# Modulation in plain fp32, four products side by side, with a new order of the first transfers, of the keys and of the second block

## The reference

```python
mod = silu(c) @ mod_w[l] + mod_b[l]           # and the same of c_ctx
shift, scale, gate = split(mod, 3)            # 1024 each
z = (rmsnorm(x, pre_g) * (1 + scale) + shift) @ w_in
y = three branches of z (attention of latents, pooling, gated linear attention)
x = x + gate * rmsnorm(merge(z, y) @ w_out, post_g)
...
x = x + rmsnorm(stick_breaking_and_relpos_attention(rmsnorm(x)))
x = x + rmsnorm(swiglu(rmsnorm(x)))
x = x + rmsnorm(recurrence(rmsnorm(x)))
x = x + rmsnorm(swiglu(rmsnorm(x)))
```

## Time and profile before

| | |
|---|---|
| median of 3 runs (lowest to highest) | 1644.01 us (1642.89 to 1644.77) |
| the profiled execution: time, span | 1642.83 us, 1641.0 us |
| TensorE busy, mean granted clock | 1507.7 us (92%), 0.963 |
| VectorE, ScalarE, GpSimd busy | 955.1, 770.3, 125.8 us |
| DMA | 212.57 MB, mean 130 GB/s |

### The profile page before, as it was taken

The page is one execution under the profiler, slowest core; times in us unless marked ns, Lnnn a source line. Parts: engine busy times, 40 slices in busy tenths (PEclk is TensorE's granted clock), DMA queues, the critical chain, the costliest instruction groups (busy, mean ns, idle before and its releaser), DMA issues.

```text
span 1641.0 us, 23866 instructions
## 1 busy us (share of the span) xinstructions
PE 1507.7 (92%) x9902; PEld 1308.2 (80%) x9902; DVE 955.1 (58%) x1522; ACT 770.3 (47%) x1212; POOL 125.8 (8%) x145
## 2 busy tenths in 40 slices
PE   6899999899999998999989886888999988889997
PEld 4767776787877775677988786877999988889997
DVE  5546875345453646576366557666566448767642
ACT  6534444432325354544535544565444358644342
POOL 0000000000000021000000013002122020122200
PEclk9999999899999999999999998999999999999999
DMA  9123333222222252322334454423666544446651
GB/s 369 64 64 116 128 103 116 77 78 77 77 77 96 84 181 85 97 90 69 99 121 137 154 185 154 131 77 103 207 192 186 187 142 142 141 149 186 193 182 63
DMA packets 58266, 212.57 MB, mean 130 GB/s; under 512 B 6384, under 2 KB 7536, under 8 KB 58032
## 3 DMA queue, kind: packets, MB, share of 16 engines
q1 hardware_dynamic: 56832, 205.29, 38.1%
q0 software_dynamic: 1328, 5.77, 1.1%
HBM read 209.98 MB, written 1.05 MB: 129 GB/s over the span
## 4 chain that ended last, share of the span: by engine, by line
PE 76%; DVE 13%; ACT 6%; DMA 3%; issue 1%; POOL 0%; SPq 0%; DVEq 0%; ACTq 0%; POOLq 0%
PE B L596 49%; PE B L612 7%; PE B L1005 7%; DVE WL L1785 4%; DMA RAW<-wstream 3%; PE B L719 3%; ACT WH L1200 3%; PE B L988 1%; PE B L1016 1%; PE B L799 1%; DVE M L2223 1%; PE B L786 1%; DVE X L2230 1%; PE B L621 1%; PE B L916 1%
## 5 line engine op out<-in xcount | busy, mean ns | idle before, releaser
L1785 DVE TENSOR_TENSOR WL<-RAW,WH 128x1024 fp32r<-128x1024 f32 x384 | 471.0, 1235 | 446.5 <-ACT WH L1200 445.5
L596 PE MATMUL B<-XH,WH 128*128 128x256 f32 (+1 forms) x1632 | 520.9, 319 | 11.4 <-ACT Z L1267 5.3
L596 PE MATMUL B<-XL,WH 128*128 128x256 f32 (+1 forms) x1632 | 505.7, 310 | 0.0
L596 PE MATMUL B<-XH,WL 128*128 128x256 f32 (+1 forms) x1632 | 505.6, 310 | 0.0
L1200 ACT ACTIVATE WH<-RAW 128x1024 fp32r<-128x1024 f32 x384 | 396.3, 1052 | 143.7 <-DMA RAW<-wstream 143.3
L596 PEld LDWEIGHTS B<-XH,WH 128*128 128x128 f32 x1632 | 313.5, 192 | 46.7 <-issue 16.6
L596 PEld LDWEIGHTS B<-XL,WH 128*128 128x128 f32 x1632 | 313.4, 192 | 20.3 <-issue 4.5
L596 PEld LDWEIGHTS B<-XH,WL 128*128 128x128 f32 x1632 | 313.1, 192 | 17.1
L612 PE MATMUL B<-XH,WH 128*128 128x256 f32 (+1 forms) x208 | 74.0, 356 | 39.5 <-DVE XL L2235 27.0
L1005 PE MATMUL B<-HH,WL 128*128 128x256 f32 x304 | 85.1, 280 | 0.0
L1005 PE MATMUL B<-HL,WH 128*128 128x256 f32 x304 | 85.1, 280 | 0.0
(11 more groups left out here) (320 smaller groups left out, 2539.3 us busy)
## 6 DMA issues: line engine op xcount, KB each, us to landing
RAW<-wstream SPq DMA_DIRECT2D x384, 512.0 KB, 3.5
X<-x_t SPq DMA_DIRECT2D x1, 2048.0 KB, 18.5
SW<-small POOLq DMA_DIRECT2D x2, 896.0 KB, 10.7
SW<-small POOLq DMA_DIRECT2D x2, 768.0 KB, 9.1
BT<-rel POOLq DMA_DIRECT2D x1, 1024.0 KB, 16.3
X<-consts POOLq DMA_DIRECT2D x1, 768.0 KB, 9.2
out_t<-X SPq DMA_DIRECT2D x3, 256.0 KB, 2.5
C<-consts SPq DMA_DIRECT2D x1, 624.0 KB, 14.1
```

The source lines that it names most:

```text
L596: last = mm(out, w, x, start=i == 0, stop=i == len(pairs) - 1)
L1785: v.tensor_tensor(lo_of(h), raw_of(h), hi_of(h).bitcast(f32), ALU.subtract).then_inc(lo_ready, 1)
```

## The change

1. Modulation's halves are not split. `mod_pair` takes two halves at once in four plain fp32 products: stationary 32 columns wide, at columns 0, 32, 64 and 96 of the array (`tile_position`), moving operand the raw half. 24 pairs: 8 at the start, 12 in the loop, 4 behind the output; a turn for every four pairs (6 in all: 2 at the start, 2 in the loop, 1 right behind it, 1 in layer 1; before there were 4, 1 of them in the loop and 1 right behind it). The counts of splits follow in `SPLITS`.
2. The first transfers come in another order, X in four pieces; the scale's rows come before the shift's, so that X is scaled before the shift is there; the first four columns run two at a time; small weights start later.
3. Keys of two heads are one product, with a weight 128 wide, and VectorE takes them out in two copies.
4. In the second block VectorE adds the mask, head by head, beside its evictions in the first eight columns; both scans stand before the evictions; ScalarE does keys before weights; scaling stands directly before its addition.

```diff
-PROJECTED = (((0, 0, "q"), (1, 0, "k"), (3, 1, "q"), (4, 1, "k")), ((0, 0, "q"), (0, 0, "k"), (1, 1, "q"), (1, 1, "k")))
+PROJECTED = (((0, 0, "q"), (1, 0, "k"), (3, 1, "q")), ((0, 0, "q"), (0, 0, "k"), (1, 1, "q")))
...
+def mod_step(p):
+    return (p - MOD_START) * 8 // 3
+def mod_halves(p):
+    quarter, rows_ = 2 * (p // 4), p % 4
+    at = [4 * (quarter + c) + rows_ for c in range(2)]
+    return [2 * PLAN["mod", 0] + a if a < 24 else 2 * PLAN["mod", 1] + a - 24 for a in at]
...
-        for j in range(MOD_FIRST):
-            place[mod_step(j) + 2].append(("m", j))
+        for p in range(MOD_START, MOD_FIRST):
+            place[mod_step(p) + 2].append(("m", p))
...
+MOD_ORDER = (4, 5, 6, 7, 0, 1, 2, 3)
...
-    group(("mod", 0), PLAN["mod", 0], 0, 16)
+    def mod_pair(p):
+        at["m", 0, p] = len(order)
+        order.extend(mod_halves(p))
+    for p in MOD_ORDER:
+        mod_pair(p)
...
+WHOLE = {AT["m", 0, p] + c for p in range(MOD_ALL) for c in range(2)}
+SPLITS = list(itertools.accumulate(int(k not in WHOLE) for k in range(HALVES)))
+def ahead(k, count):
+    return next((j for j in range(k + 1, k + 3) if SPLITS[j] == SPLITS[k] + count), k + 3)
...
-        return [0, 1, 2, 3, 4, 5, 6, 7, 13, 14, 15, 16]
+        return [0, 1, 2, 3, 5, 13, 14, 15, 16]
...
+        CV = [sb(f"CV{i}", a, KT, 32) for i, a in enumerate((kb(109), kb(134), kb(127)))]
+        MROW = [sb(f"MROW{i}", a, 512) for i, a in enumerate((kb(103), kb(138), kb(78)))]
...
             sp.dma_start(V[:, :], vecs).then_inc(v_in, 16)
-            for k in range(12):
+            for k in range(2):
                 half(k)
-            sp.dma_start(C[:, :], consts).then_inc(c_in, 16)
-            sp.dma_start(X[:, :, :], x_t).then_inc(x_in, 16)
-            for k in range(12, HALVES):
+            sp.dma_start(C[:, 0:C_MASK], consts[:, 0:C_MASK]).then_inc(c_in, 16)
+            for k in range(2, 8):
+                half(k)
+            for i, arrived in enumerate(x_in):
+                sp.dma_start(X[:, 2 * i:2 * i + 2, :], x_t[:, 2 * i:2 * i + 2, :]).then_inc(arrived, 16)
+            half(z0)
+            half(z0 + 1)
+            for k in range(8, z0):
+                half(k)
+            half(z0 + 2)
+            half(z0 + 3)
+            sp.dma_start(C[:, C_MASK:], consts[:, C_MASK:]).then_inc(const_in, 16)
+            for k in range(z0 + 4, HALVES):
                 half(k)
...
-            pool.wait_ge(halves_done, 12)
+            pool.wait_ge(halves_done, AT["z", 0, FIRST[1]] + 1)
...
-            pool.wait_ge(bias_in, 48)
-            p.tensor_tensor(BT[:, :, 0:P], BT[:, :, 0:P], causal_neg[:, 0, 0:P].unsqueeze(1).to_broadcast([P, HEADS, P]), ALU.add)
-            p.tensor_tensor(BT[:, :, P:TW], BT[:, :, P:TW], causal_neg[:, 1, :].unsqueeze(1).to_broadcast([P, HEADS, SEQ]),
-                            ALU.add).then_inc(bt_ready, 1)
...
-                            pe.wait_ge(lo_ready, k0 + h + 1)
+                            pe.wait_ge(lo_ready, SPLITS[k0 + h])
...
-            def mod_half(k, i, bank, cr):
-                pe.wait_ge(lo_ready, k + 1)
+            def mod_pair(p, bank, cv):
+                k = AT["m", 0, p]
+                for h in range(k, k + 2):
+                    pe.wait_ge(raw_in[SLOT[h]], 16 * NTH[h])
                 for j in range(2):
-                    kt = 2 * i + j
-                    mm(bank[:, :], cr[:, kt, :], hi_of(k)[:, j * 512:(j + 1) * 512], start=kt == 0, stop=False)
-                    last = mm(bank[:, :], cr[:, kt, :], lo_of(k)[:, j * 512:(j + 1) * 512], start=False, stop=kt == KT - 1)
-                last.then_inc(halves_done, 1)
+                    for c in range(2):
+                        at = 32 * (2 * c + j)
+                        last = mm(bank[at:at + 32, :], cv[:, 2 * (p % 4) + j, :], raw_of(k + c)[:, j * 512:(j + 1) * 512],
+                                  start=p % 4 == 0, stop=p % 4 == 3, tile_position=(0, at))
+                last.then_inc(halves_done, 2)
...
-                    pe.wait_ge(cl_ready, 1)
-                    for c in range(4):
-                        bank = take(c, "mod", c)
-                        for i in range(4):
-                            mod_half(4 * c + i, i, bank, CR0)
-                        if c == 2:
-                            pe.wait_ge(c_in, 16)
+                    pe.wait_ge(cv_ready, 1)
+                    pe.wait_ge(c_in, 16)
+                    pe.wait_ge(select_ready, 1)
+                    for s in (1, 0):
+                        bank = take(s, "m", s)
+                        for p in range(4 * s, 4 * s + 4):
+                            mod_pair(p, bank, CV[0])
+                        bank = take(4 + 2 * s, "turn", s)
+                        taken_out("m", s)
+                        mod_turn(bank, MROW[0]).then_inc(sel_ready, 1)
+                        if s == 1:
                             residual_sum(0)
-                    bank = take(4, "turn")
-                    for c in range(4):
-                        taken_out("mod", c)
-                    mod_turn(bank, MROW[:, :]).then_inc(sel_ready, 1)
...
+                together = 2 if l == 0 else 4
+                for i in range(0, 4, together):
+                    for kt in some_columns(AT["z", l, FIRST[i]], outs[i:i + together],
+                                           lambda kt, h: XH[:, kt, tokens(l, FIRST[i + h])],
+                                           lambda kt, h: XL[:, kt, tokens(l, FIRST[i + h])], range(KT)):
+                        if i == 0:
+                            pe.wait_ge(xl_ready, n.next(xl_ready))
...
-                    projected(product(ring_take("k", l, h)[0:NOPE, :], [(SW[:, SW_MORE + SW_UK + h * NOPE:SW_MORE + SW_UK + (h + 1) * NOPE], Z[:, Z_KV, :])]),
+                    projected(product(ring_take("k", l, h)[:, :], [(SW[:, SW_MORE + SW_UK + h * NOPE:SW_MORE + SW_UK + (h + 2) * NOPE], Z[:, Z_KV, :])]),
...
-                    if l == 0 and u == 21:
-                        modulation_turn(0)
+                    if l == 0 and u - 3 in ROWS_AT:
+                        modulation_turn(ROWS_AT[u - 3])
...
                 if l == 0:
-                    modulation_turn(1)
+                    modulation_turn(4)
...
-                    pe.wait_ge(cl_ready, 3)
-                    for j in range(MOD_FIRST, MOD_ALL):
-                        bank = take(6 + (j - MOD_FIRST) // 4, "m", j // 4) if j % 4 == 0 else bank
-                        mod_half(AT["m", 0, j], j % 4, bank, CR2)
+                    pe.wait_ge(cv_ready, 3)
+                    bank = take(6, "m", 5)
+                    for p in range(MOD_FIRST, MOD_ALL):
+                        mod_pair(p, bank, CV[2])
...
+                while split[0] <= min(k, HALVES - 1):
+                    h = split[0]
+                    split[0] += 1
+                    if h not in WHOLE:
+                        act.wait_ge(raw_in[SLOT[h]], 16 * NTH[h])
+                        A(hi_of(h), raw_of(h), ACT.Copy).then_inc(hi_ready, 1)
...
-                    hi_upto(11)
-                    act.wait_ge(x_in, 16)
                     for k in range(0, KT, 2):
+                        act.wait_ge(x_in[k // 2], 16)
                         A(SQ[:, k:k + 2, :], X[:, k:k + 2, :], ACT.Square).then_inc(sq_ready, 1)
-                        hi_upto(12 + k // 2)
+                    hi_upto(AT["z", 0, FIRST[1]])
                     residual_root(0)
-                    hi_upto(AT["z", 0, FIRST[-1]])
+                    act.wait_ge(shift_ready, 1)
...
+                    if l == 0 and k in (2, 5):
+                        hi_upto(AT["z", 0, FIRST[2 + k // 4]])
...
+                        n4, n5 = banks.n[4], banks.n[5]
                         filled(FILLED[g + 1][0])
-                        weights(h, banks.n[4])
                         if g >= 0:
                             keys(2 * g)
-                        weights(h + 1, banks.n[5])
-                        if g >= 0:
                             keys(2 * g + 1)
+                        weights(h, n4)
+                        weights(h + 1, n5)
...
+                    def mod_row(s):
+                        dve.wait_ge(halves_done, AT["m", 0, 4 * s + 3] + 2)
+                        v.tensor_copy(MROW[0][:, :], bank_of("m", s)[:, :]).then_inc(free("m", s), 1)
                     mod_row(1)
+                    wait(sel_ready)
+                    mod_group(1, bank_of("turn", 1)).then_inc(free("turn", 1), 1)
+                    taken_out("turn", 1)
+                    link(gain_before(0))
+                    lo_upto(AT["z", 0, FIRST[1]])
+                    wait(rstd_ready)
+                    for k in range(KT):
+                        scaled(0, k)
+                        if k == 3:
+                            mod_row(0)
+                    wait(sel_ready)
+                    mod_group(0, bank_of("turn", 0)).then_inc(free("turn", 0), 1)
+                    taken_out("turn", 0)
```

(43 more changed lines are left out.)

182 lines of the change are left out of this document (74 added, 108 removed).

## The result

The changed kernel takes 1620.58 us (median of 4 runs, 1617.67 to 1621.56) against 1644.04 us; the ratio is 0.9848, with a 95% interval of 0.9831 to 0.9865. Run once more later, it gave 1620.26 us and 0.9867 (0.9847 to 0.9887). I had said 1612 in a range of 1603 to 1626: faster, as forecast, but by 23.5 us in place of 32.

The account below looks back on a forecast made before the run. TensorE, busy 92% of the span, was taken to bound the kernel. The terms summed to -32.3 us: 1642.8 to 1610.5 us, with 1.2 to the median 1611.7, said as 1612, range 1603 to 1626.

Parts of the forecast that it names:

- Side by side: Modulation in the first layer's loop: four products at once, 1.02 us a pair, 12 pairs replacing 24 halves, -10.3 us.
- Start: New transfer order and unsplit halves bring the first input product from 46.50 to about 41 us, -5.5 us.
- Keys: Both layers' loops: eight fewer key products at 1.0 us each, -8.0 us, half of it in each loop.
- Boundary and scans: Entering the second block without GpSimd's mask adds, -6.4 us; its attention with both scans before the evictions, -6.0 us.
- one split less before 280.66, -1.2: Loop: TensorE's 3.10 us wait for the gate's product, behind a VectorE split, shortens by 1.2 us.
- +1.1 for one more turn: In or right behind the loop: three turns of rows into columns in place of two, +1.1 us.
- given back +3: Allowance of 3 us, bounds 0 and +8, for waits that appear where TensorE gets shorter.
- Behind the output product: After the first layer's output: eight halves become four pairs, but the last half's landing gates them, 0 us.
- two abreast: Rival: only two modulation products overlap, 1.88 us a pair, total 1624 us; chance 0.12.
- serial: Rival: modulation products run one after another, 3.60 us a pair, total 1652 us; chance 0.03.
- the start and the scans: Two rivals: the start gives nothing, 1617.5 us, chance 0.10; the scans' order gives nothing, 1618 us, chance 0.09.
- the main case: Whole kernel: all terms hold, 1612 us, spanning 1604 to 1619 by itself; chance 0.60.

Follow-up runs that it names:

- experiment 4: Changed kernel with three of every four modulation pairs multiplied in the same 32 array columns, sums not kept: 1650.87 us, ratio 1.0054.
- experiment 11: Changed kernel with one head's keys to a product, as before, 16 products in place of 8: 1634.20 us (1624.13 to 1639.42), ratio 0.9945.
- experiment 5: Changed kernel with the second block's attention in its old order of scans and of ScalarE's keys: 1629.76 us, ratio 0.9908.
- experiment 8: Changed kernel with half 16 split late, small weights late, loop turns one unit later, and scaling a chunk ahead of its addition again: 1605.87 us, ratio 0.9761.
- experiment 9: Changed kernel with both halves of a loop modulation pair landing in one slot: 1615.23 us, ratio 0.9829.
- experiment 3: Changed kernel with the loop's two turns of modulation rows one unit later, on TensorE and VectorE: 1615.36 us, ratio 0.9832.
- experiment 6: Changed kernel with the mask added to the bias on GpSimd at the boundary, as before: 1627.47 us, ratio 0.9891.
- experiment 7: Changed kernel with half 16 split late, small weights late and loop turns one unit later: 1605.95 us, ratio 0.9764.
- experiment 10: Changed kernel with half 16 split late, small weights late, loop turns one unit later, and both pair halves in one slot: 1602.80 us, ratio 0.9755.

## Why the prediction came out as it did

- **Side by side.** Right in mechanism and size: 1.00 us a pair against 1.02, taken from two products abreast; experiment 4 shows 3.55 us for the other case, against my 3.60. My other estimate, 1.12 us a pair, was too high.
- **Start.** Right; each event within 1 us, 7.4 gained in place of 5.5: the first input product came 6.4 us sooner, and the half clock ended 2.7 us behind it (at 42.85), in place of 5.1 (to 51.6).
- **Keys.** In layer 1's loop each of the four missing products is a step of 1.0 us in the difference of starts. The layer as a whole gained 1.5 us of these 4 (0.6 to 4.8 in the other traces); the waits that took the rest were not looked into. The total stays unsettled by experiment 11.
- **Boundary and scans.** Right in mechanism, 7.1 in place of 6.4 and 8.2 in place of 6.0 (9.6 by experiment 5). The attention's waits cost more than their own length, in part because some of what follows them runs at half clock; I had priced them at their length. The term of +1.0 for scaling directly before adding measured nothing (experiment 8).
- **Loop.** The term "one split less before 280.66, -1.2" had the wrong sign: the stall grew from 3.10 to 4.83. I looked at the split on VectorE and not at what fed it; the pair holds two of four slots, and the next split half is issued late (experiment 9). The +1.1 for one more turn (my text says "Two more turns", but three where there were two is one more, and the sum counts one) left out the bank that the turn takes from the ring: 4.8 us, 2.98 of them waiting (experiment 3). Against these stands the wait that fell from 2.88 to 0.36, with 0.69 just ahead of it, which I had not counted. My "given back +3" was a guess without a place; the loop fell short of 14.4 by 3.3 us in the first trace and by 4.7 to 6.5 in the others.
- **Behind the output product: the term that failed.** I wrote "The last half's landing still gates the pairs. So 0 (bounds -1 and +1)". It cost 8.4, and 6.8 to 8.7 in the other traces. The half that gates TensorE here is not the last modulation half but the one behind it, half 16, and its landing moved. The removed splits were what had held ScalarE back: before, its copies waited 4.43 and 3.26 us for modulation halves there, and its evictions, GpSimd's sum and GpSimd's small weights followed late, behind half 16. With the splits gone ScalarE was early, GpSimd's 1.7 MB were issued first, and the half that everything waited for took 10.1 us in place of 4.4. I had listed GpSimd's queue at the start, where the change touches it by name, and not here, where it is reached through the sum.
- **The end.** 1.0 forecast to be lost, 5.3 and 4.9 measured, about half of it in the stretch of the recurrence (2.9 and 2.6). In experiments 6, 7, 9, 10 and 11 that stretch loses only 0.2 or less, with the same code and a granted clock of 0.94 in place of 0.90. What makes the clock differ between them stays open; no run was made for it.

The rivals: two abreast and serial are excluded by the 1.00 us; the start and the scans both gave more than nothing. What came was the main case with waits of 8 us and more, to which I had given 0.05. That the time still lies in my range owes something to luck: start, boundary and attention gave 4.8 us more than their terms, which paid for half of the 8.4.

## What to carry to other kernels

When work is taken off an engine that isn't the bound, follow its queue to the next transfer it triggers, through other engines too, and ask which urgent transfer will now share the DMA engines with it; here one wait of one instruction in front of a bulk transfer was worth 6 us. When an edit takes a bank, a slot or another place in a ring, count the ring: a turn of 1 us cost almost another 5 through its bank. And where operands arrive whole, room kept for their split parts is room for another transfer.

## What the runs showed of the hardware that I had not expected

- Four plain fp32 products with 32 stationary columns each, at four positions, take 0.99 to 1.00 us from the first to the next instruction, as long as one product (two passes, 0.86) and 0.14: no loss for the fourth, and no more for entering and leaving than the weighing's 0.16. Behind the output product, where pairs follow one another, two start 0.86 us apart (607.02 and 607.88): the 0.14 is paid once for a run of pairs.
- An idle stretch of TensorE can cost more than itself. Behind the new 2.98 us the clock granted from 171 to 180 us was 0.81, at 1.2 GHz in part, and around the 7.11 us (590 to 597) it was 0.58 from 590 to 605. Taking the first away moved the products after it by 4.8 us.
- The half of 512 KB landed in 4.3 to 4.4 us, and in 10.1 with 1.7 MB issued just ahead of it from GpSimd.
